# The activations and all that lies behind them moved by 64 bytes against the weight buffers

## The reference

```python
def reference(x, ...):
    x = first_block(x, ...)      # layer 0: RG-LRU and windowed attention; layer 1: retention
    return second_block(x, ...)  # 2 x (FFN, three attentions with gates, FFN)

h = h + _mixer(_rmsnorm(h, gain), ...)                     # first block, per layer
h = h + _swiglu(_rmsnorm(h, ffn_norm[l]), w_gu, w_down)    # (silu(h@wg) * (h@wu)) @ wd, width 2816
x = x + 0.5 * rms_norm(swiglu(rms_norm(x, g), wg, wu, wd), g_post)   # second block, twice per layer
x = x + rms_norm(hybrid_mixer(rms_norm(x, g_mix_pre[l]), w_in[l], ...), g_mix_post[l])
```

## Time and profile before

| | |
|---|---|
| median of three runs | 2012.21 us (2011.77 to 2013.87) |
| profiled execution, its span | 2011.9 us |
| PE busy with matmuls | 1998.7 us, 11810 matmuls |
| DVE busy | 1178.9 us |
| ACT busy | 990.8 us |
| mean granted clock of TensorE | 0.997 |
| weights read | 341.10 MB |

### The profile page before, as it was taken

One profiled execution on the slowest core, in us unless ns is written; L12 is line 12 of the kernel. 1 busy time (PEld: TensorE's weight loads), 2 busy tenths in 40 slices (PEclk: granted clock), 3 DMA queues, 4 the chain that ended last, 5 costly groups with the idle time before them and its releaser, 6 DMA issues.

```text
span 2011.9 us, 27800 instructions
## 1 busy us (share of the span) xinstructions
PE 1998.7 (99%) x11810; PEld 1755.0 (87%) x11810; DVE 1178.9 (59%) x1133; ACT 990.8 (49%) x1076; POOL 303.7 (15%) x204
## 2 busy tenths in 40 slices
PE   9999999999999999999999999999999999999998
PEld 8899999999999988887888888888888888888887
DVE  6854446757654455546566865546555556686553
ACT  6753334345544354445356564446444535666443
POOL 4034401514344010002100110001000210011000
PEclk9999999999999999999999999999999999999999
DMA  7345556544555555554543445554556554354553
GB/s 223 105 138 176 167 179 201 168 129 144 186 177 181 188 187 184 185 197 159 176 147 126 167 168 188 188 209 159 185 180 209 168 167 146 112 209 154 183 180 136
DMA packets 195587, 343.67 MB, mean 171 GB/s; under 512 B 14122, under 2 KB 97356, under 8 KB 195356
## 3 DMA queue, kind: packets, MB, share of 16 engines
q1 hardware_dynamic: 194844, 340.12, 51.3%
q0 software_dynamic: 368, 0.79, 0.2%
q10 hardware_dynamic: 272, 1.26, 0.2%
HBM read 341.10 MB, written 1.05 MB: 170 GB/s over the span
## 4 chain that ended last, share of the span: by engine, by line
PE 91%; DVE 4%; ACT 3%; DMA 1%; POOL 1%; issue 0%; SPq 0%; DVEq 0%; POOLq 0%; ACTq 0%
PE banks L557 18%; PE banks L560 17%; PE banks L558 17%; PE banks L397 7%; PE banks L399 7%; PE banks L398 7%; PE banks L448 5%; PE banks L1778 2%; PE banks L1779 2%; PE banks L1780 2%; DVE w_lo L391 1%; PE banks L596 1%; PE banks L1869 1%; PE banks L1871 1%; PE banks L1870 1%; ACT w_hi L375 1%
## 5 line engine op out<-in xcount | busy, mean ns | idle before, releaser
L391 DVE TENSOR_TENSOR w_lo<-raw,w_hi 128x2048 fp32r<-128x2048 f32 x307 | 730.5, 2382 | 514.5 <-ACT w_hi L375 514.0
L375 ACT ACTIVATE w_hi<-raw 128x2048 fp32r<-128x2048 f32 x311 | 593.8, 1913 | 648.3 <-DMA raw<-ffn_wd 149.6
L557 PE MATMUL banks<-w_hi,xn_hi 128*128 128x512 f32 x1192 | 471.9, 396 | 0.9 <-DVE xn_lo L818 0.5
L558 PE MATMUL banks<-w_lo,xn_hi 128*128 128x512 f32 x1192 | 464.1, 389 | 0.0
L560 PE MATMUL banks<-w_hi,xn_lo 128*128 128x512 f32 x1192 | 459.6, 390 | 0.0
L557 PEld LDWEIGHTS banks<-w_hi,xn_hi 128*128 128x128 f32 x1192 | 223.9, 188 | 49.3 <-DVE w_lo L391 3.0
L560 PEld LDWEIGHTS banks<-w_hi,xn_lo 128*128 128x128 f32 x1192 | 223.8, 188 | 47.6
L558 PEld LDWEIGHTS banks<-w_lo,xn_hi 128*128 128x128 f32 x1192 | 224.1, 188 | 44.0
L397 PE MATMUL banks<-xn_hi,w_hi 128*128 128x272 f32 (+1 forms) x720 | 208.4, 289 | 0.5 <-DVE w_lo L1162 0.5
L399 PE MATMUL banks<-xn_hi,w_lo 128*128 128x272 f32 (+1 forms) x720 | 207.1, 288 | 0.0
L398 PE MATMUL banks<-xn_lo,w_hi 128*128 128x272 f32 (+1 forms) x720 | 206.7, 287 | 0.0
(11 more groups left out here) (371 smaller groups left out, 3079.1 us busy)
## 6 DMA issues: line engine op xcount, KB each, us to landing
raw<-w_in SPq DMA_DIRECT2D x58, 1024.0 KB, 5.1
raw<-ffn_wd SPq DMA_DIRECT2D x44, 1024.0 KB, 4.8
raw<-ffn_w_gu SPq DMA_DIRECT2D x42, 1024.0 KB, 4.9
raw<-ffn_wu SPq DMA_DIRECT2D x40, 1024.0 KB, 5.0
raw<-ffn_wg SPq DMA_DIRECT2D x35, 1024.0 KB, 5.0
raw<-ret_w_in SPq DMA_DIRECT2D x24, 1024.0 KB, 5.1
raw<-ffn_w_down SPq DMA_DIRECT2D x22, 1024.0 KB, 4.8
raw<-ret_w_out SPq DMA_DIRECT2D x8, 1024.0 KB, 5.4
```

What stands on the lines that cost most here:

```text
L375: nc.scalar.activation(hi_of(n0), raw_of(n0), ACT.Copy).then_inc(hi_done(n0), 1)
L391: nc.vector.tensor_tensor(lo_of(n0), raw_of(n0), hi_of(n0).bitcast(F32), ALU.subtract).then_inc(lo_done(n0), 1)
L557: pe.matmul(ps[:, (b + n) * 512:(b + n + 1) * 512], xh, h, start=start, stop=False)
L558: pe.matmul(ps[:, (b + n) * 512:(b + n + 1) * 512], xh, o, start=False, stop=False)
```

## The change

The tiles `hT`, `xn_hi`, `xn_lo`, `act_hi`, `act_lo`, `Y` and everything behind or inside them start 64 bytes later: phase 64 instead of 0. The ring of weights stays. The own buffers `raw_x`, `lo_x`, `hi_x`, which lie inside `Y` and `act_hi`, get an offset of 448 more and so stay on multiples of 512. The two staging buffers `stage0` and `stage1` of the first FFN go along with `act_hi`. No instruction is added, removed or moved: on each of the five engines the order of the instructions is that of before, only line numbers rise by one behind line 45 and by two behind line 201.

```diff
 SLOTS = 4
 AHEAD = 2
+A_PHASE = 64
 CH = 2048
@@
             if name in ("act_hi", "act_lo"):
-                at[0] += (raw_at - at[0]) % 512
+                at[0] += (hT_at - at[0]) % 512
             return place(name, shape, dt, off), off
@@
         w_hi, _ = new("w_hi", [P, SLOTS, CH], F32R)
-        hT, _ = new("hT", [P, KT, T1])
+        at[0] += A_PHASE
+        hT, hT_at = new("hT", [P, KT, T1])
         xn_hi, xn_at = new("xn_hi", [P, KT * T1], F32R)
@@
         raw_x, lo_x, hi_x = ([place(f"{name}{b}", [P, CH], dt, at0 + off) for b, at0 in enumerate((extra_at, a_at))]
-                             for name, dt, off in (("raw_x", F32, 0), ("lo_x", F32R, 0), ("hi_x", F32R, 4 * CH)))
+                             for name, dt, off in (("raw_x", F32, 512 - A_PHASE), ("lo_x", F32R, 512 - A_PHASE), ("hi_x", F32R, 512 - A_PHASE + 4 * CH)))
```

## The result

The changed kernel is slower. Its median is 2035.91 us (2035.56 to 2037.36, four runs), that of the kernel before 2011.99 us (2011.77 to 2013.87, four runs). The ratio is 1.0118, with a 95% interval of 1.0105 to 1.013. The forecast was 1976.6 us with a range of 1964 to 2014: the kernel moved the other way, and its time lies outside the range.

What follows compares the result with a forecast made beforehand. PE's own matmul work was taken to bound the kernel: 33.9 (second block) + 2.7 (second FFN) - 1.0 (late next) = 35.6 us off 2011.9 gives 1976.3, median 1976.6 us, range 1964 to 2014.

Steps and rivals of the forecast that it cites:

- PE alone bounds the time, and the change reaches only what stands on top of the columns: Whole kernel: only PE's own work sets the time; 13.3 ns per matmul beyond its columns' streaming time is all that can change.
- Only the distance between the two operands' phases counts: Second block, 512 columns: streaming 0 against stationary 64 acts like phase 192, 6.7 ns on top instead of 13.3.
- Rival B: Second block: opposite sign, stationary 64 acts like streaming 64; gain 11.4 us in all, 2000.8 us; chance 0.22.
- Second block: 5088 matmuls of 512 columns, stationary operand moved to phase 64: 220.0 ns each, a gain of 33.9 us.
- A steady run behaves as the six in a row at phase 192: First block, 256 columns: the last three of six took 113.3 ns each, 6.7 on top, carried over to 5088 matmuls.
- Rival C: Second block: nothing gained, a steady run at one phase settles at 13.3 ns on top; 2009.5 to 2012.2 us; chance 0.14.
- Second FFN, 256 columns: First block: streaming operand goes from phase 0 to 64; 1584 matmuls gain 1.7 ns each, 2.7 us.
- First block, the rest: Slices go round all four phases before and after, so 0; where the round isn't whole, 0.8 us either way.
- Late next: Five product ends in the second block: PE reaches unshortened ACT and DVE chains sooner, some 0.2 us each, 1 us lost.
- Rival D: Second block: slower, the stream overtakes a load starting one 64-byte piece ahead; costs 17.3 us, 2026.8 us; chance 0.13.
- one 0.13 us step: First block, 272 columns, 150.87 to 151.00: dearest single distance, 16.7 ns on top, used as bound for a 17.3 us loss.

Runs made afterwards that it cites:

- different openings: Separate kernel, not a reference computation: 36 equal matmuls behind each of six short preceding runs; 256 columns streaming from 64 took 113.3 ns once, 117.8 five times.
- the series agree: Kernels of their own, computing nothing of the reference: series of 48 or 36 equal float32r matmuls, phases and column count set per series.
- the map: Separate kernel, not a reference computation: series of 48 equal matmuls per phase pair; 226.7 to 234.3 ns at 512 columns, 113.3 to 120.1 at 256.

## Why the prediction was wrong, step by step

- *PE alone bounds the time, and the change reaches only what stands on top of the columns.* Right. The 22.2 us lie in the distances between matmuls; splits took as long as before, and the two waits of PE that moved, +1.5 and -0.8 us, nearly cancel.
- *Only the distance between the two operands' phases counts.* Right as far as tried: with both at 64 the kernel takes the time of before, 1.0002. That stationary 64 stands for streaming 192 was right too: at 512 columns the two take 233.1 each from series to series, and streaming 64 (228.8) is as dear as stationary 192 (229.0). Rival B would have been no better, since distance +64 at 512 columns isn't cheap either (228.8 to 229.0).
- *Second block: "I take the first, because the length of the load is the same 128 columns there, and because 13.3 was the same at 256 and 512 columns."* **This is the step that failed.** It carried a price from 256 columns over to 512. That 13.3 stands on top of both is true of distance 0 and of that alone. At -64 it is 6.7 or 11.1 on top of 256 columns and 20 on top of 512. Forecast -33.9 us, measured +26.7. So the part of the stream beyond the load is not free of cost: what stands on top of the columns depends on the column count and the distance together.
- *A steady run behaves as the six in a row at phase 192.* Also weak: a pair can have several rates, and phase 192 at 256 columns fell back to 117.8 in the whole kernel. Phase 64 and phase 192 were each seen at both 113.3 and 117.8 behind different openings, so that the 5 ns between them in the earlier trace rows need not be a matter of the phase at all. The row itself was also read at its best end. The 113.3 are the last three of a run of six, which begins at 317.88; all six take 0.69 us, 115.0 ns each. The six behind it, from 318.57 to 319.28, stream from phase 0 and take 0.71, 118.3 ns each and not 120.0:

```profile
317.88 0.28 PE L1778 MATMUL banks<-xn_hi,w_hi 128*128 128x256 f32 x1
...
319.28 0.28 PE L1778 MATMUL banks<-xn_hi,w_hi 128*128 128x256 f32 x1
```

  Within that chunk phase 192 is 3.3 ns cheaper than phase 0, half of the 6.7 that went into the sum. Rival C doubted that such a rate lasts, though it expected 13.3 to come back, which it didn't.
- *Second FFN, 256 columns: -2.7 us.* Right in kind, too small in size: -3.6 us, the twelve matmuls in 1.42 us as forecast. The sum over the group fell by 2.3 ns for each, 120.0 to 117.8 for most.
- *First block, the rest: 0, 0.8 us either way.* 272 columns in the first FFN gained 1.2 us, a little outside, of which 0.7 may be chance, since the kernel with everything at 64 gained that much there with the distances of before; each line of the retention products moved by 0.3 or less.
- *Late next, 1 us lost at the ends of products.* Never came up, since PE reached them later, not earlier.
- *Rival D, slower, 2026.8.* Its direction and its place were right, its size was not: it took 3.4 ns a matmul from one 0.13 us step at 272 columns, and the steady loss is 6.6 ns. The mean loss is smaller, 26.7 us / 5087 = 5.3: distances of up to 245 ns rose from 227.3 to 233.3 on the mean, and the longer ones, where waits and transposes break the series, add up to 40.4 us (121 of them) instead of 45.3 (129). Its reason, that the stream overtakes a load which starts one piece ahead of it, was not tested by anything here. It had a chance of 0.13; the rows of before did not exclude it, and there was no row of a stationary operand off 0 with 512 columns. That lack called for nearly even chances of both signs.
- The Trainium skill, "TensorE: Matmul & The Clock Gate", section "Step-by-step: what each phase is for", speaks of two independent read ports. At 320 columns the series agree with that, 146.6 ns at stationary phases 0, 64 and 192; at 256 (113.3 to 120.1) and 512 columns (226.7 to 234.3) they don't.

What stays open is the mechanism: why a given pair has these rates and not others, and by what a break picks one of them. That the stream and the next load disturb each other in SBUF, as the forecast took it, fits the dependence on the distance, but no run here shows it. The runs give the prices, not the reason.

## What to carry to other kernels

Where PE bounds a kernel of float32r matmuls and they follow each other without a gap, each with its own weight load, the distance between the start addresses of the streaming and the stationary operand, modulo 256, moves a matmul of 256 columns by up to 6% and one of 512 by up to 3%. Measure it at the kernel's own column count and behind several openings: a price from another count can have the wrong sign, and one from a single or a short series the wrong size. Prefer a distance that keeps a low rate behind different openings (0 at 512 columns, 112 at 256) to one that was the best in a single series, and shift operands per stage, inside their buffers, rather than all at once.

## What the runs showed of the hardware that I had not expected

- One pair of addresses and one length can run at several steady rates: 113.3, 116.7 and 118.7 ns at 256 columns and distance 16, 226.7 and 233.3 at 512 columns and a stationary operand at 16. A rate is kept for tens of microseconds; in the whole kernel with `xn` and `act` at 16 it changed 49 times, only where something broke the series.
- With 512 columns no distance on the map went below 226.7 ns, 13.3 on top of the columns at 2.4 GHz. With 256 the least was 113.3, 6.7 on top. The two commonest rates of 512 columns, 226.7 and 233.3, are 6.7 ns apart, 16 clocks at the granted 2.4 GHz.
- Sixteen more columns may turn the sign of one and the same shift: at 400 columns the stationary operand at 64 costs 3.3 ns (180.0 to 183.3), at 416 it gains 1.5 (188.2 to 186.7), and at 464 it costs 4.4 again (208.9 to 213.3). These are single series, so another opening might give other prices.
